# Twelve sums of normed activation rows for the first MLP product made by GpSimd instead of VectorE

## What is computed

```
merged = sigmoid(gate_a) * y_a + sigmoid(gate_b) * y_b
x = x + merged @ w_out
h2 = rms_norm(x, norm_mlp_g)
x = x + square(relu(h2 @ w_mlp1)) @ w_mlp2
```

## Time and profile before

| what | value |
|---|---|
| time, median of 3 runs | 2645.11 us (2644.02 to 2645.84) |
| the profiled execution: its own time | 2645.87 us |
| its span in the profile | 2644.2 us |
| PE busy | 2593.9 us, 98% |
| DVE busy | 1425.3 us, 54% |
| ACT busy | 1094.3 us, 41% |
| POOL busy | 244.5 us, 9% |
| granted TensorE clock, mean | 0.995 |

### The profile page before, as it was taken

How to read it: one execution, slowest core, us unless ns; L and a number is a source line. 1 busy time by engine, 2 the same in 40 slices (tenths; PEclk the granted TensorE clock), 3 DMA queues, 4 the chain that set the end, 5 groups by cost and what they waited for, 6 DMA issues and landing times.

```text
span 2644.2 us, 40459 instructions
## 1 busy us (share of the span) xinstructions
PE 2593.9 (98%) x15434; PEld 2352.9 (89%) x15434; DVE 1425.3 (54%) x2196; ACT 1094.3 (41%) x1784; POOL 244.5 (9%) x407
## 2 busy tenths in 40 slices
PE   7999999999999999999999999999999799999998
PEld 6888888888888888888888888899999799999887
DVE  4335542354333633336443353988888677677843
ACT  5554245542454425544343334633343233333621
POOL 3000000100001000010010011011111210000000
PEclk9999999999999999999999999999999899999999
DMA  3122121221222212122163233234434772452022
GB/s 115 25 33 63 53 70 26 36 70 38 73 33 26 80 39 70 25 34 73 44 247 103 99 109 121 71 132 138 148 127 138 251 228 97 147 164 80 25 68 60
DMA packets 218603, 236.44 MB, mean 89 GB/s; under 512 B 15440, under 2 KB 189072, under 8 KB 218416
## 3 DMA queue, kind: packets, MB, share of 16 engines
q0 software_dynamic: 34576, 138.78, 16.3%
q1 hardware_dynamic: 181760, 95.05, 13.6%
q10 hardware_dynamic: 2080, 0.14, 0.1%
HBM read 168.73 MB, written 65.02 MB: 88 GB/s over the span
## 4 chain that ended last, share of the span: by engine, by line
PE 94%; DVE 3%; DMA 2%; issue 1%; ACT 0%; SPq 0%; POOL 0%; DVEq 0%; ACTq 0%; POOLq 0%
PE banks L1085 18%; PE banks L1087 18%; PE banks L1086 18%; PE banks L1444 5%; PE banks L1445 5%; PE banks L1446 5%; PE banks L1375 5%; PE banks L1373 5%; PE banks L1374 5%; PE banks L1200 2%; PE banks L1181 1%; PE banks L1283 1%; PE banks L1270 1%; PE banks L1191 1%; DMA w_raw<-in_w_mlp_dram 1%
## 5 line engine op out<-in xcount | busy, mean ns | idle before, releaser
L1085 PE MATMUL banks<-act_hi,w_hi 128*128 128x512 f32 (+1 forms) x2424 | 903.1, 373 | 0.7 <-DVE act_lo L2075 0.7
L1087 PE MATMUL banks<-act_hi,w_lo 128*128 128x512 f32 (+1 forms) x2424 | 860.3, 355 | 0.0
L1086 PE MATMUL banks<-act_lo,w_hi 128*128 128x512 f32 (+1 forms) x2424 | 859.1, 354 | 0.0
L1087 PEld LDWEIGHTS banks<-act_hi,w_lo 128*128 128x128 f32 x2424 | 457.3, 189 | 66.3
L1085 PEld LDWEIGHTS banks<-act_hi,w_hi 128*128 128x128 f32 x2424 | 458.5, 189 | 57.5 <-DVE act_lo L2075 0.9
L1086 PEld LDWEIGHTS banks<-act_lo,w_hi 128*128 128x128 f32 x2424 | 459.4, 190 | 53.8
L1444 PE MATMUL banks<-op,ring 128*128 128x320 f32 x896 | 278.4, 311 | 16.2 <-issue 15.6
L1722 ACT ACTIVATE work<-banks 128x512 f32<-128x512 f32 (+4 forms) x228 | 113.4, 505 | 426.3 <-PE banks L1087 425.9
L1445 PE MATMUL banks<-op,ring 128*128 128x320 f32 x896 | 278.0, 310 | 0.0
L1446 PE MATMUL banks<-op,ring 128*128 128x320 f32 x896 | 278.0, 310 | 0.0
L2050 DVE TENSOR_TENSOR w_lo<-w_raw,w_hi 128x1024 fp32r<-128x1024 f32 (+1 forms) x111 | 131.4, 1184 | 144.5 <-ACT w_hi L1528 143.6
(11 more groups left out here) (349 smaller groups left out, 4232.2 us busy)
## 6 DMA issues: line engine op xcount, KB each, us to landing
w_raw<-in_w_in_dram SPq DMA_DIRECT2D x76, 512.0 KB
operand_scratch<-work POOLq DMA_DIRECT2D x112, 320.0 KB, 2.7
op_f<-operand_scratch POOLq DMA_DIRECT2D x28, 1280.0 KB, 6.5
w_raw<-in_w_mlp_dram SPq DMA_DIRECT2D x64, 256.0 KB, 5.3
work<-gate_scratch POOLq DMA_DIRECT2D x16, 640.0 KB, 5.5
gate_scratch<-work POOLq DMA_DIRECT2D x15, 640.0 KB, 3.3
w_raw<-in_w_mlp_dram SPq DMA_DIRECT2D x16, 512.0 KB, 4.4
raw<-in_w_mlp_dram SPq DMA_DIRECT2D x16, 512.0 KB, 5.6
```

The source lines that it names most:

```text
L1085: nc.tensor.matmul(out, wh, rh, start=first and k == 0, stop=False, skip_group_check=True)
L1086: nc.tensor.matmul(out, wh, rl, start=False, stop=False, skip_group_check=True)
L1087: mm = nc.tensor.matmul(out, wl, rh, start=False, stop=k == kt - 1, skip_group_check=True)
```

## The change

The twelve sums for m = 1, 7, 6 leave DVE's steps 0, 1 and 2 and are issued by POOL, in the same order and with the same inputs, outputs and semaphore. POOL first waits for the last product of the output projection (`mm_done`), for the last part of the scaled rows (`h_ready`) and for DVE's first eight sums (`xs_sum` at 9, since it starts at 1).

```diff
@@ POOL, behind the stores of the output projection's rows @@
+            def piece_sum(m, a):
+                (k0, f0), (k1, f1) = x_rows(m, a)
+                nc.gpsimd.tensor_tensor(x_sum_at(m, a), h_half(k0, f0), h_half(k1, f1), ALU.add).then_inc(xs_sum, 1)
+
+            pool.wait_ge(mm_done, slab_chunks(N_D) + 1)
+            pool.wait_ge(h_ready, KT + 3)
+            pool.wait_ge(xs_sum, 9)
+            for m in (1, 7, 6):
+                for pair in range(4):
+                    piece_sum(m, pair)
@@ DVE, loop over g @@
-                if g < 3:
-                    for pair in range(4):
-                        piece_sum((1, 7, 6)[g], pair)
-                elif g < 7:
+                if 3 <= g < 7:
                     for pair in range(4):
                         piece_low((5, 1, 7, 6)[g - 3], pair)
```

## The result

The change makes the kernel slower: 2651.7 us, median of 9 runs (2650.53 to 2654.78), against 2644.47 for the kernel before in 9 runs (2643.25 to 2647.11). The ratio is 1.0026 with a 95% interval of 1.0016 to 1.0035, that is 4.2 to 9.3 us. The profiled execution took 2651.81 us, its span is 2650.3.

What follows compares the result with a forecast made beforehand. PE was busy 98% of the span, with DVE the bound from 1689 to 1704.4. A chain 7.0 us late, with freed DVE time worth 0, took profiled 2645.9 to 2652.9, or 2652.1 against the median; range 2648.6 to 2656.5.

Steps and rivals of the forecast that it cites:

- POOL's step: Each POOL sum of 640 elements adds 1.48 us; twelve make 17.8 us from 1665.9.
- Exclusion: POOL waits out DVE instructions with two SBUF inputs; five of them between 1665.9 and POOL's end charge it 3.2 us.
- rival A: No exclusion between POOL and DVE: POOL ends at 1683.7, chain 3.8 us late, time 2648.9; chance 0.2.
- POOL's end: POOL's last of twelve sums, which ScalarE's first copy for product 6 awaits: 1683.7 + 3.2 = 1686.9.
- DVE held by POOL: Before products 2 to 5, DVE waits up to one POOL sum per instruction; nothing charged.
- cover: Product 2's residuals end by about 1670.4, before PE's 1672.09; weight sums of 3 to 5 are wanted from 1675.79.
- Rival C: DVE starved until POOL finishes; PE stalls before product 2, product 6's weight sum 9.9 us late, time 2655; chance 0.07.
- The wait and the chain: ScalarE's copies for product 6 wait for POOL's last sum, making DVE's work through product 9's weight residual 7.0 us late.
- The freed DVE time: The 8.8 us of DVE issue freed by the sums lies before the wait and is worth 0.
- Gaps and clock: PE gap of about 6 us before product 6, 1 to 3 us at 8 and 9; product 6's low clock covered.
- Rival D: Low clock lasts longer behind the 6 us gap: products 6 to 8 at 1.2 GHz throughout, time 2655; chance 0.06.
- Rival B: POOL sums near DVE's pace; chain keeps its place at 1.16 us, 3.2 us sooner at 0.74, time 2642; chance 0.04.

Runs made afterwards that it cites:

- e4: The changed kernel, but VectorE writes zeros in place of the weight sums of products 3 to 5; 2650.63 us, ratio 1.0020 to the kernel before.
- e5: The changed kernel, but POOL writes zeros in place of the twelve sums, which are left out; 2641.61 us, ratio 0.9987 to the kernel before.
- e3: The changed kernel, but POOL makes only the eight sums of m = 7 and 6, DVE the four of m = 1; 2649.32 us, ratio 1.0013.
- e1: The changed kernel, but ScalarE's copy for product 6 of each pair waits for that pair's sums alone, not all twelve; 2650.6 us, ratio 1.0021.
- e6: On top of e1, the split of m = 1 goes ahead of that of m = 5 on ScalarE and DVE; 2650.7 us, ratio 1.0021.
- e2: The changed kernel, but POOL makes only the four sums of m = 6, DVE the eight of m = 1 and 7; 2646.76 us, ratio 1.0006.
- b2: The kernel before, with DVE's residuals of m = 6 moved from step 6 to 9 and of m = 7 from step 5 to 7; 2643.61 us, ratio 0.9995.

## Why the prediction was right

Forecast 2652.1 us, measured 2651.7; the change's mechanism is the one forecast. That the two numbers agree within 0.4 us is in part luck: the interval of the measured change is 5 us wide, and an exclusion charged 0.7 us too high stands against a step taken 0.2 too low in the sum of twelve, and the low clock behind the new gap, longer than forecast, could be absorbed. Step by step:

**POOL's step.** 1.48 us by the rows of 128 and 256 elements; the four undisturbed sums take 1.50. It began at 1665.84, taken as 1665.9.

**Exclusion.** Charged 3.2 us as the full length of five DVE instructions; the rows give 2.5 (1686.35 - 1665.84 - 12 x 1.50), about 0.5 us for each and not their full 0.61 to 0.74. The one pair of rows from the kernel before had been read as whole-length exclusion. The pair, a POOL sum and a DVE instruction, takes 2.0 us where the two alone take 1.50 and 0.61 from start to start, so a little of them does overlap. e4 showed that it is these instructions, and e5, where POOL only writes, shows no hold-up of DVE; rival A (POOL's end at 1683.7) is refuted. POOL's end: forecast 1686.9, measured 1686.35.

**DVE held by POOL.** I had no row for this half and charged nothing because of cover. That held: product 2 started at 1671.96 without a gap, product 3 at 1675.67. Rival C, a DVE that gets no turn until POOL is through, is refuted by the alternation: DVE's weight residual ended at 1670.0, with the 1670.4 that the prediction allowed. e3 shows how near the edge was: with four sums left on DVE the same cover fails and PE stands 4.69 us.

**The wait and the chain.** First copy forecast 1687.0, measured 1686.44; residual 0.76 us behind it (0.77); weight sum of product 6 forecast 1690.7, measured 1690.15. Chain forecast 7.0 us late, 6.6 by the rows. No run leaves all twelve sums on POOL and takes the wait away altogether; that the wait is what carries the loss rests on these rows, on e1 and on e5.

**The freed DVE time** was set at 0, and it is 0: 8.98 us of idling in front of product 6's residuals. e6 adds that filling it with other residuals won nothing either.

**Gaps and clock.** In front of product 6 about 6 us were forecast, 5.27 measured; at product 8 0.68 and at 9 3.01, where 1 to 3 was said. Product 6 was set at 5.16 us, as product 9 before, and lasted 5.72, since its low clock held for 4.5 us; at full clock it had lasted 3.75. The 0.68 us of waiting left at product 8 shows that this was covered. Rival D is refuted: product 6 ran at 0.267 us a matmul from 1694.0 to about 1698.5 and at 0.147 behind it. Rival B needed 1.16 us a sum, and the sums take 1.50. Its figure of 3.2 us sooner doesn't follow from the rows it names (1683.66 - 1680.1 is 3.6); e5 measured 3.2, and there DVE's own residuals set the place, not product 3's end.

**The size.** The chain's 6.6 us and the medians' 7.2 us agree within what a comparison of this kernel can tell (the interval is 4.2 to 9.3). The rest of 0.6 us is not assigned.

## What to carry to other kernels

Work given to an idle engine is priced by who waits for its last piece, not by the time it frees on the busy one: twelve additions freed 8.8 us of VectorE that could not be used, and made VectorE's queue 6.6 us late through a wait for all twelve on a third engine. GpSimd additions that read SBUF were no parallel help to a VectorE running instructions with two SBUF inputs: here each pair took 2.0 us, and VectorE alone would have done both in about 1.35 (0.735 + 0.61). What did relieve VectorE was its own order: residuals and sums moved behind those that PE wants sooner, with no work taken away, gave 4.7 us.

## What had not been expected of the hardware

In this stretch VectorE and GpSimd alternate, one instruction each, while both have instructions with two SBUF inputs ready, and both rows are stretched in the profile: VectorE's weight sum from 0.68 to 2.0 us, GpSimd's sum from 1.53 to 2.1. The waiting is booked as busy time: VectorE's total fell by 3.9 us only (1425.3 to 1421.4) though 8.8 us of issue had left it. The low clock doesn't always come right at a gap's end: behind the gap of 5.27 us PE restarts at 1.2 GHz, but behind the 3.01 us one in the same kernel the first matmuls follow at 0.147 us, the low level begins 1.4 us later (1712.3) and lasts 3.4 us, about as in the kernel before, where it began at once. Nor does the length of the gap decide it: in e1 a gap of 3.02 us was followed by a granted clock of 1.00 throughout, in e3 one of 2.12 us by 0.66 (1708 to 1713), while gaps of 2.04 us (e2, at product 8) and 1.88 us (b2) left it at 1.00. A forecast that charges a gap with a fixed loss of clock can be off by about 1.5 us in either direction.
